# A group of products split in three, state-space chunks five tiles apart, and bias loads moved behind the last chunk's inputs

## The chip, the cores and the metric

The kernel runs on one core of a Trainium2 chip. The metric is the device time of one execution in microseconds. A core has five engines that run their own instruction streams and meet at semaphores: TensorE (PE, with its weight loads as PEld), VectorE (DVE), ScalarE (ACT), GpSimd (POOL), and SyncE (SP), which here only issues DMAs. ScalarE issues a few DMAs too.

## The reference, cut to what matters

Two transformer blocks over 256 tokens of 2048 channels, all in float32. The first block projects the normed input into queries, keys and values of a neighbourhood attention, a state-space input and memory queries; the three mixers' outputs are normed, joined and projected, and an MLP follows. The second block has four other mixers, its own out-projection and MLP.

```python
proj = h @ w_in                       # h = rmsnorm(x), 256 x 2048
q_na, k_na, v_na, u_ssm, q_mem = split(proj, [1024, 2048, 3072, 3584])
# neighbourhood attention: scores + bias table na_rpb, window 8 x 16 of a 64-wide grid
s = einsum('bqhd,bqkhd->bhqk', q_blk, k_g) * scale + rpb_flat[:, bidx]
# state space, 32 groups x 64 states, both directions: h_t = lam_bar * h_(t-1) + b_bar u_t
bu = einsum('bsgc,gpc->bsgp', u, b_bar)
_, h = associative_scan(combine, (a, bu), reverse=reverse)
y  = einsum('bsgp,gcp->bsgc', h, c).real
y  = gelu(y_f + y_b + d * u); y = y * sigmoid(y @ w_glu + b_glu)
# memory attention: q_mem against keys and values of 256 memory rows
x = x + rmsnorm(concat(norm(y_na), norm(y_ssm), norm(y_mem)) @ w_out)
x = x + rmsnorm(square(relu(rmsnorm(x) @ w_ff1)) @ w_ff2)
```

## The kernel before

Everything is one program with an order written out by hand for each engine. Weights stream through a ring of four 1 MB slots (`raw_weights`), loaded by SP in the order of `STREAM`. A product is done in one of two ways. **Unsplit** (`group`): float32 weights straight from the ring. **Split** (`group3`, `split_group`): ScalarE rounds a slot (`round_slot`, two halves, into `w_high`), VectorE takes the rest (`low`, two halves, into `w_low`), and PE does three products for each, high by high, low by high and high by low; x must be split too (`x_rounded` on ScalarE, `x_lower` on VectorE). `w_high` and `w_low` hold two slots each.

A group of 512 columns has 16 tiles of K, four to a slot. The first block's groups after the state-space input u come in this order, with the tiles counted through:

| tiles | group | form before |
|---|---|---|
| 0 to 15 | q0 | unsplit |
| 16 to 31 | k0 | unsplit |
| 32 to 47 | qm (memory queries) | unsplit |
| 48 to 63 | q1 | split |
| 64 to 79 | k1 | split |
| 80 to 111 | v0, v1 | split |

Between tiles PE calls `steps()`, which fits in the state space's work and the attention units. The state space runs in eight chunks i: `bu(i)` on PE after tile 2 + 6i; VectorE turns its result with sine and cosine tables, scans two parts of 512 (L2688), and turns back (h(i)); `ssm_y(i)` on PE; `yev(i)` on VectorE. bu(i) waits for yev(i-2), the scans for `decays(i)` on ScalarE, which waits for the scans of i-1; `tables(i)` on ScalarE waits for h(i-2) and for GpSimd's `turns`. y(i) stands after tiles 11, 17, ... 41, then 49 and 58. After y(7) come a gelu (VectorE, a tanh on ScalarE) and the gate's product.

`na_loads` on ScalarE issues 17 DMAs: a mask, and 16 pieces of the bias table of 128 KB each in rows of 64 floats, into `na_bias`, which lies over the residual. GpSimd then adds the mask to the eight heads' bias (L2080). VectorE first reads the result at attention unit 4, whose step is after tile 86.

ScalarE's order around these, before:

```python
angles(4); na_loads(); decays(2); tables(3)
...
tables(7); x_rounded(0); x_rounded(1); round_slot("q1", 0); decays(7)
act.wait_ge(pe_done, at("bu", CHUNKS - 1))
round_slot("q1", 1); x_rounded(2); x_rounded(3); evac("qm", qm)
```

The out-projections (`wout1`, `wout2`) begin with half slots (`left_half`), each over both token tiles, between which the last attention steps run; the first one waits, token tile by token tile, for the evacuation of the accumulators that it overwrites. After wout1 and ff2_1 the rows are copied out, squared and summed (`row_sums` on both engines), and PE turns them with a diagonal that ScalarE makes (L1451, PE's L832).

Of the kernel before, what the change touches and what calls it, by code (L numbers as in the profile page):

```python
# [7 lines left out]
P = 128  # L8
TT = S // P
# [14 lines left out]
CHUNKS = 8  # L24
HT = S // 2
# [30 lines left out]
STREAM += [(g, 4, False, 1) for g in ("q0", "k0", "qm")]  # L56
STREAM += [("q1", 4, True, 1), ("k1", 4, True, 1), ("glu", 1, False, 1), ("v0", 4, True, 1), ("v1", 4, True, 1), ("wout1", 16, True, 0), ("ff1_1", 64, True, 16), ("ff2_1", 64, True, 0)]
# [75 lines left out]
def program(nc, A, out, seen, book):  # L133
# [5 lines left out]
    with ctx:  # L139
# [48 lines left out]
        bbarE, cdE = tiles(place("x_behind", 22528, 2048), 0, 16, P), R(16640, 64, 32)  # L188
# [4 lines left out]
        angle = [tuple(tiles(scratch, 6144 + 1024 * b + 512 * i, 4, HT) for i in range(2)) for b in range(2)]  # L193
# [4 lines left out]
        na_mask = region[:, 1024:1536]  # L198
# [394 lines left out]
        PERIOD = 6  # L593
# [7 lines left out]
        def _(pe):  # L601
# [87 lines left out]
            def split_group(name, form="wide", between=None):  # L689

                acc_free(name)
                for j in range(KT // SK):
                    k = SPLIT_OF[SLOT0[name] + j]
                    state["n"] += 1
                    if name == "q1":
# [305 lines left out]
            def left_half(k, n, pos, first, free=None, order=(0, 1)):  # L1001
# [3 lines left out]
                for t in order:  # L1005
                    if free is not None:
                        pe.wait_ge(*free[t])
                    for c in range(2):
                        last = out_product(pos, t, c, wh[:, 512 * c:512 * c + 512], wl[:, 512 * c:512 * c + 512], first)
                last.then_inc(*((half_done, 1) if n == 0 else (split_used, 1)))  # L1010

# [32 lines left out]
            def wout1():  # L1044

                k, a0 = SPLIT0["wout1"], ACC0["wout1"]

                def scores_read():
                    pe.wait_ge(dve_done, at("scaled", U1 - 1))

                def last_value():
                    attend1(U1 + 2)

                def near_sums():
                    pe.wait_ge(act_done, at("out", U1 - 1))
# [8 lines left out]
                left_half(k, 0, 0, True, [(acc_freed, a0), (acc_freed, a0 - 1)], (1, 0))  # L1064
                attend1(U1 - 1)
                left_half(k, 1, 1, False)
                attend1(U1)
                left_half(k + 1, 0, 2, False)
                attend1(U1 + 1)
                left_half(k + 1, 1, 3, False)  # L1070
# [116 lines left out]
            for g in ("q0", "k0", "qm"):  # L1187
                group(g, xn, between=steps)
            for g in ("q1", "k1"):
                split_group(g, between=steps)  # L1190
# [157 lines left out]
            def wout2():  # L1348

                k = SPLIT0["wout2"]  # L1350

                def scores_read():
                    pe.wait_ge(dve_done, at("window", "sumread"))

                def nothing():
                    pass

                def forget_sums():
                    pe.wait_ge(act_done, at("out2", ND - 1))
# [6 lines left out]
                left_half(k, 0, 0, True, [(act_done, at("evac", "fva")), (act_done, at("evac", "fvb"))])  # L1366
                duo_step(TAIL0)
                pe.wait_ge(dve_done, at("scaled2", ND - 1))
                norm("window", xo, [gathered("window", 0, 4), gathered("window", 1, 8)], bank=4)
                left_half(k, 1, 1, False)  # L1370
# [24 lines left out]
        def _(act):  # L1395
# [57 lines left out]
            def row_sums(name, product):  # L1453

                row_copy(name, product, 0, 1, True)
                row_copy(name, product, 0, 3, True)
                row_root(name, 0)
                row_copy(name, product, 1, 1, True)
# [280 lines left out]
            acc_done("memv")  # L1739
            angles(0)  # L1740
# [35 lines left out]
            def na_loads():  # L1776

                act.wait_ge(dve_done, at("x", "out"))
                act.wait_ge(dve_done, at("cd_stepped"))
# [26 lines left out]
            na_loads()  # L1806
# [30 lines left out]
            evac("q1", q1[:, 4:8])  # L1837
# [264 lines left out]
        def _(dve):  # L2102
# [49 lines left out]
            def row_sums(name, product, after, eps=None):  # L2152

                row_copy(name, product, 0, 0, True)
                slot_half(after, 0, 0)
                row_copy(name, product, 0, 2, True)
                row_factor(name, 0, eps)
                row_copy(name, product, 1, 0, True)
                row_copy(name, product, 1, 2, True)
                row_factor(name, 1, eps)  # L2160

            def row_copies(name, product, after):

                row_copy(name, product, 0, 0, False)
                slot_half(after, 0, 0)
                row_copy(name, product, 0, 2, False)
                row_copy(name, product, 1, 0, False)
                row_copy(name, product, 1, 2, False)

# [487 lines left out]
            def x_lower(c):  # L2657

                dve.wait_ge(act_done, at("x", "high", c))
                dve.wait_ge(pe_done, at("slot", SLOT0["qm"] + c))  # L2660
# [40 lines left out]
            x_lower(2)  # L2701
            low("q1", 2)
            x_lower(3)
# [172 lines left out]
            for (g, j), (nxt, q) in zip(WOVEN_SLOTS, AHEAD):  # L2876
                ticks = TICKS[g, j]
                for slot, name, x in ((("sq", 1), "nq", nq), (("fk", 1), "fq", fq)):
                    if (g, j) == slot:
                        dve.wait_ge(act_done, at("evac", name))  # L2880
                        tt(x, x, by_keys(4), ALU.mult, name + "_scaled")
                for c, p in enumerate(ticks):
# [8 lines left out]
                    duo_normal(p)  # L2891
                    if p == FOX0:
# [120 lines left out]
```

## Time and profile before

| | |
|---|---|
| median of 3 runs | 2266.74 us (2266.41 to 2266.82) |
| the profiled execution's own time | 2266.6 us |
| its span | 2264.8 us |
| PE busy | 2238.2 us, 99% |
| VectorE, ScalarE busy | 1332.2 us (59%), 1040.4 us (46%) |
| GpSimd busy | 94.0 us (4%) |
| granted clock of PE | 1.00 of full speed in the whole span |
| 50 to 300 us: busy in each 50 us | PE 49.52, 50.00, 50.00, 50.00, 50.00; VectorE 45.03, 41.39, 41.63, 35.13, 26.43 |

A busy time is the union of an engine's instructions. Matmuls overlap, so the step from one to the next is the time that one costs, not its own duration. "[3.38 <-PE ps L914]" behind an instruction says that its engine was idle for 3.38 us before it and what ended the wait. "ACTq" and "SPq" are the queues' DMA issues.

### The profile page before, as it was taken

The page shows a single profiled execution, that of the slowest core. Times are in us where ns is not written, and L with a number is a line of the kernel's source. Part 1 is how long each engine was busy: PE and PEld are TensorE (multiplying, and loading weights), DVE is VectorE, ACT ScalarE, POOL GpSimd, SP SyncE. Part 2 cuts the span into 40 slices and gives each one's busy share as a digit, 9 for nine tenths or more (in the row PEclk, how much of TensorE's full clock was granted, in tenths as well). Part 3 has the DMA queues.
Part 4 walks back from the last instruction along what each step waited for, and adds up shares of the span by engine and source line. Part 5 has one row for each costly group of instructions (what it writes and reads, how often), then busy time and mean ns, then how long its engine had stood idle before and what let it go on. Part 6 is the DMA issues. An engine that isn't in the chain of part 4 may idle for free.

```text
span 2264.8 us, 32839 instructions
## 1 busy us (share of the span) xinstructions
PE 2238.2 (99%) x13276; PEld 1918.9 (85%) x13276; DVE 1332.2 (59%) x1548; ACT 1040.4 (46%) x1453; POOL 94.0 (4%) x66
## 2 busy tenths in 40 slices
PE   8999999999999999999999999999999999999998
PEld 7888988888888888888898988888888888888887
DVE  6878665764545545444486578847545455454445
ACT  6433564543434444444464466636434344444444
POOL 0552000000000000000000000000000000000000
PEclk9999999999999999999999999999999999999999
DMA  8364436566666555565544433355666665555553
GB/s 322 128 155 153 149 130 228 154 186 185 185 185 185 187 196 193 206 239 186 195 158 139 165 113 113 131 195 158 186 185 185 185 185 187 202 186 194 194 188 109
DMA packets 153513, 402.32 MB, mean 178 GB/s; under 512 B 15296, under 2 KB 30912, under 8 KB 133200
## 3 DMA queue, kind: packets, MB, share of 16 engines
q1 hardware_dynamic: 142112, 394.83, 53.0%
q10 hardware_dynamic: 11312, 6.22, 1.2%
q8 instruction: 65, 1.06, 0.2%
q14 instruction: 24, 0.20, 0.0%
HBM read 398.90 MB, written 2.13 MB: 177 GB/s over the span
## 4 chain that ended last, share of the span: by engine, by line
PE 93%; DVE 4%; ACT 2%; issue 1%; DMA 0%; SPq 0%; ACTq 0%; DVEq 0%
PE ps L757 21%; PE ps L758 11%; PE ps L795 10%; PE ps L797 10%; PE ps L796 10%; PE ps L620 5%; PE ps L628 3%; PE ps L629 3%; PE ps L630 3%; PE ps L997 2%; PE ps L999 2%; PE ps L998 2%; PE ps L642 1%; PE ps L644 1%; PE ps L643 1%
## 5 line engine op out<-in xcount | busy, mean ns | idle before, releaser
L2284 DVE TENSOR_TENSOR w_low<-raw_weights,w_high 128x1024 fp32r<-128x1024 f32 x659 | 776.4, 1218 | 782.5 <-ACT w_high L1487 778.3
L1487 ACT ACTIVATE w_high<-raw_weights 128x1024 fp32r<-128x1024 f32 (+1 forms) x634 | 634.7, 1049 | 817.0 <-PE ps L797 398.5
L757 PE MATMUL ps<-x_split,w_high 128*128 128x512 f32 x2048 | 725.3, 399 | 1.7 <-DVE x_split L2272 1.7
L758 PE MATMUL ps<-x_split,w_low 128*128 128x256 f32 x2048 | 575.2, 281 | 0.0
L757 PEld LDWEIGHTS ps<-x_split,w_high 128*128 128x128 f32 x2048 | 384.8, 188 | 98.4 <-issue 3.0
L795 PE MATMUL ps<-w_high,x_split 128*128 128x512 f32 x1024 | 398.4, 389 | 0.0
L797 PE MATMUL ps<-w_high,x_split 128*128 128x512 f32 x1024 | 398.4, 389 | 0.0
L796 PE MATMUL ps<-w_low,x_split 128*128 128x512 f32 x1024 | 398.4, 389 | 0.0
L758 PEld LDWEIGHTS ps<-x_split,w_low 128*128 128x128 f32 x2048 | 386.9, 189 | 0.0
L797 PEld LDWEIGHTS ps<-w_high,x_split 128*128 128x128 f32 x1024 | 192.3, 188 | 40.2
L796 PEld LDWEIGHTS ps<-w_low,x_split 128*128 128x128 f32 x1024 | 192.3, 188 | 39.7
L795 PEld LDWEIGHTS ps<-w_high,x_split 128*128 128x128 f32 x1024 | 192.3, 188 | 39.7
L629 PE MATMUL ps<-x_split,w_high 128*128 128x256 f32 x544 | 153.8, 283 | 0.0
L628 PE MATMUL ps<-x_split,w_high 128*128 128x256 f32 x416 | 121.4, 292 | 0.8 <-DVE x_split L2272 0.4
L630 PE MATMUL ps<-x_split,w_low 128*128 128x256 f32 x416 | 117.5, 283 | 0.0
L620 PE MATMUL ps<-x_over_high,raw_weights 128*128 128x256 f32 x512 | 115.0, 382 | 0.0
L620 PEld LDWEIGHTS ps<-x_over_high,raw_weights 128*128 128x128 f32 x512 | 95.9, 190 | 14.6 <-issue 1.2
L629 PEld LDWEIGHTS ps<-x_split,w_high 128*128 128x128 f32 x544 | 104.2, 192 | 0.2
L997 PE MATMUL ps<-w_high,x_split 128*128 128x512 f32 x256 | 101.4, 396 | 2.8 <-ACT region L1926 1.6
L999 PE MATMUL ps<-w_high,x_split 128*128 128x512 f32 x256 | 99.7, 390 | 0.0
L998 PE MATMUL ps<-w_low,x_split 128*128 128x512 f32 x256 | 99.7, 389 | 0.0
L1523 ACT ACTIVATE region<-ps 128x1024 f32 (+1 forms) x32 | 32.9, 1027 | 116.1 <-PE ps L758 116.1
(298 smaller groups left out, 2321.5 us busy)
## 6 DMA issues: line engine op xcount, KB each, us to landing
raw_weights<-in_w_ff SPq DMA_DIRECT2D x128, 1024.0 KB, 5.6
raw_weights<-in_w_up SPq DMA_DIRECT2D x64, 1024.0 KB, 5.7
raw_weights<-in_w_down SPq DMA_DIRECT2D x64, 1024.0 KB, 4.8
raw_weights<-in_w_in SPq DMA_DIRECT2D x62, 1024.0 KB, 5.4
raw_weights<-in_w_out SPq DMA_DIRECT2D x32, 1024.0 KB, 4.8
raw_weights<-in_w_mem_kv SPq DMA_DIRECT2D x7, 1024.0 KB, 14.6
residual<-in_xT SPq DMA_DIRECT2D x2, 2048.0 KB, 14.4
region<-t_table ACTq DMA_DIRECT2D x1, 3072.0 KB, 16.6
```

The costliest lines, as they stand in the source:

```text
L620: last = nc.tensor.matmul(acc[:, c], w[:, P * c:P * c + P], x, start=(kt == 0 and c % 2 == 0), stop=(kt == kts - 1), skip_group_check=True)
L628: nc.tensor.matmul(o, h, xh_, start=(first and c % 2 == 0), stop=False, skip_group_check=True)
L629: nc.tensor.matmul(o, h, xl_, start=False, stop=False, skip_group_check=True)
L630: last = nc.tensor.matmul(o, wl[:, P * c:P * c + P], xh_, start=False, stop=done, skip_group_check=True)
L757: nc.tensor.matmul(o, wh[:, q, w], xs[:, kt], start=(kt == 0), stop=False, skip_group_check=True)
L758: last = nc.tensor.matmul(o[:, 0:S], wl[:, q, w], xh[:, kt], start=False, stop=(kt == KT - 1), skip_group_check=True)
L795: nc.tensor.matmul(o, h, wh[:, r], start=(first and j == 0), stop=False, skip_group_check=True)
L796: nc.tensor.matmul(o, h, wl[:, r], start=False, stop=False, skip_group_check=True)
L797: last = nc.tensor.matmul(o, l, wh[:, r], start=False, stop=True, skip_group_check=True)
L997: nc.tensor.matmul(o, h, wh, start=first, stop=False, skip_group_check=True)
L1487: nc.scalar.activation(split_slot(wh_t, k)[:, r], ring_slot(n)[:, r], ACT.Copy).then_inc(rounded, 1)
L2284: V.tensor_tensor(split_slot(wl_t, k)[:, r], ring_slot(n)[:, r], split_slot(wh_t, k)[:, r].bitcast(f32), ALU.subtract).then_inc(split_read ...
```

## The change

The memory queries' group (qm) becomes a split group. Its x is therefore split earlier, in place over xn as k0's slots are used up, and high x goes where `bbarE` was; `bbarE` and the angles move into the residual's place. With that, `na_loads` can only run when the last `bu` is done. The chunks' steps are listed anew: bu after 2, 7, 12, 17, 22, 27, 37, 47, y after 10, 15, 20, 25, 31, 42, 53, 62. Three more edits stand further on: both out-projections begin with `first_rows`, which does two half slots for one token tile and only then asks for the second accumulator; the half slot that VectorE lowers amid the row copies moves behind them, and ScalarE copies one more row piece ahead of the first root; the scaling of nq and fq moves behind a tick's normalising.

```diff
-STREAM += [(g, 4, False, 1) for g in ("q0", "k0", "qm")]
-STREAM += [("q1", 4, True, 1), ("k1", 4, True, 1), ...
+STREAM += [(g, 4, False, 1) for g in ("q0", "k0")]
+STREAM += [("qm", 4, True, 1), ("q1", 4, True, 1), ("k1", 4, True, 1), ...
...
-        bbarE, cdE = tiles(place("x_behind", 22528, 2048), 0, 16, P), R(16640, 64, 32)
+        bbarE, cdE = tiles(xres_t, 0, 16, P), R(16640, 64, 32)
-        angle = [tuple(tiles(scratch, 6144 + 1024 * b + 512 * i, 4, HT) ...
+        angle = [tuple(tiles(xres_t, 2048 + 1024 * b + 512 * i, 4, HT) ...
-        na_mask = region[:, 1024:1536]
+        na_mask = mix_t[:, 1024:1536]
...
-        BU_AFTER = {2 + PERIOD * i: i for i in range(CHUNKS)}
-        Y_AFTER = {**{11 + PERIOD * i: i for i in range(CHUNKS - 2)}, 49: CHUNKS - 2, 58: CHUNKS - 1}
+        BU_AFTER = dict(zip((2, 7, 12, 17, 22, 27, 37, 47), range(CHUNKS)))
+        Y_AFTER = dict(zip((10, 15, 20, 25, 31, 42, 53, 62), range(CHUNKS)))
...
+            def first_rows(k, order, free, between):
+                for i, t in enumerate(order):
+                    pe.wait_ge(*free[t])
+                    for n in range(2):
+                        if i == 0:
+                            pe.wait_ge(split_ready, 2 * k + n + 1)
+                        wh, wl = (split_slot(x, k)[:, HALF * n:HALF * n + HALF] for x in (wh_t, wl_t))
+                        for c in range(2):
+                            last = out_product(n, t, c, ..., n == 0)
+                    if i == 0:
+                        last.then_inc(half_done, 1)
+                        between()
+                last.then_inc(split_used, 1)
...
             # ScalarE
             acc_done("memv")
+            act.wait_ge(dve_done, at("x", "out"))
...
             angles(4)
-            na_loads()
             decays(2)
...
             angles(6)
+            for c in range(4):
+                x_rounded(c)
             decays(4)
             tables(5)
             angles(7)
+            round_slot("qm", 0)
             decays(5)
+            round_slot("qm", 1)
             tables(6)
             evac("k0", k1[:, 0:4])
+            round_slot("qm", 2)
             decays(6)
+            round_slot("qm", 3)
             tables(7)
-            x_rounded(0)
-            x_rounded(1)
             round_slot("q1", 0)
+            act.wait_ge(pe_done, at("bu", CHUNKS - 1))
+            na_loads()
+            evac("qm", qm)
+            round_slot("q1", 1)
             decays(7)
-            act.wait_ge(pe_done, at("bu", CHUNKS - 1))
-            round_slot("q1", 1)
-            x_rounded(2)
-            x_rounded(3)
-            evac("qm", qm)
             round_slot("q1", 2)
             round_slot("q1", 3)
             round_slot("k1", 0)
+            evac("q1", q1[:, 4:8])
             act.wait_ge(dve_done, at("gelu_in"))
             ... Tanh ...
-            act.wait_ge(pool_done, at("na_masked"))
-            evac("q1", q1[:, 4:8])
...
             # VectorE, chunk loop
+                if i == CHUNKS - 3:
+                    x_lower(0)
+                    low("qm", 0)
+                if i == CHUNKS - 2:
+                    x_lower(1)
+                    low("qm", 1)
+                    x_lower(2)
+                    low("qm", 2)
                 if i == CHUNKS - 1:
-                    x_lower(0)
                     low("q1", 0)
...
                     (scans of chunk i)
+                if i == CHUNKS - 2:
+                    x_lower(3)
+                    low("qm", 3)
                 if i == CHUNKS - 1:
-                    x_lower(1)
                     low("q1", 1)
                 if i:
                     yev(i - 1)
```

## Rows read from the trace of the kernel before

**Rows 1.** The page, busy times; and a group's total and mean ns of one.

```profile
PE 2238.2 (99%) x13276; PEld 1918.9 (85%) x13276; DVE 1332.2 (59%) x1548; ACT 1040.4 (46%) x1453; POOL 94.0 (4%) x66
...
L1487 ACT ACTIVATE w_high<-raw_weights 128x1024 fp32r<-128x1024 f32 (+1 forms) x634 | 634.7, 1049 | 817.0 <-PE ps L797 398.5
```

**Rows 2.** PE's waits, whole span: us in total, times, longest.

```profile
PE ps L628 <- DVE mem_low L2514: 7.6, 1, 7.6
PE ps L832 <- ACT rinv L1451: 3.7, 4, 1.3
...
PE ps L997 <- ACT region L1926: 1.6, 1, 1.6
PE ps L1110 <- DVE region L2445: 1.1, 1, 1.1
PE ps L997 <- ACT region L1513: 0.8, 1, 0.8
```

**Rows 3.** Chain that ended last, 150 to 250 us: start, us, what.

```profile
176.24 5.38 PE ps L620 x24
181.61 1.14 PE ps L914 x32
...
188.13 0.36 PE ps L928 x8
188.50 1.88 PE ps L934 x64
...
204.41 0.12 PE ps L628
...
204.65 0.12 PE ps L630
```

**Rows 4.** Timeline of VectorE, 60 to 175 us: start, us, what.

```profile
117.02 2.63 DVE L2688 TENSOR_TENSOR_SCAN mixed<-mixed 128x512 f32<-128x512 f32 x2
...
154.56 1.29 DVE L2107 TENSOR_TENSOR region<-ps,region 128x512 f32<-128x512 f32 x2 [3.21 <-PE ps L914]
...
159.06 2.34 DVE L2688 TENSOR_TENSOR_SCAN region<-mixed,region 128x512 f32<-128x512 f32 x2
...
164.02 1.29 DVE L2107 TENSOR_TENSOR region<-region 128x512 f32<-128x512 f32 x2
168.69 1.29 DVE L2107 TENSOR_TENSOR region<-ps,region 128x512 f32<-128x512 f32 x2 [3.38 <-PE ps L914]
```

**Rows 5.** Timeline of ScalarE and its queue, 60 to 260 us.

```profile
111.69 0.33 ACTq L1780 DMA_DIRECT2D region<-in_na_mask  x1
...
114.84 13.30 ACTq L1786 DMA_DIRECT2D residual<-in_na_rpb  x12
128.19 0.63 ACT L1768 ACTIVATE mixed<-rinv 128x508 f32<-128x508 f32 x1 [13.44 <-DVE region L2107]
```

**Rows 6.** The line of the bias loads: ns min/median/max.

```profile
L1786 ACTq DMA_DIRECT2D residual<-in_na_rpb x16: 642/672/3517, 112.1 to 127.5; - x16
```

**Rows 7.** Timelines of GpSimd and VectorE, 166 to 290 us.

```profile
171.37 13.95 POOL L2080 TENSOR_TENSOR residual<-residual,region 128x512 f32<-128x512 f32 x8
...
173.22 4.33 DVE L2688 TENSOR_TENSOR_SCAN mixed<-mixed 128x512 f32<-128x512 f32 x2
...
180.86 3.31 DVE L2107 TENSOR_TENSOR mixed<-region,mixed 128x512 f32<-128x512 f32 x2
```

**Rows 8.** Timelines of VectorE and ScalarE, 222 to 233 us.

```profile
222.82 0.42 DVE L2107 TENSOR_TENSOR mixed<-ps,mixed 128x256 f32<-128x256 f32 x1 [3.07 <-PE ps L934]
225.57 2.36 DVE L2284 TENSOR_TENSOR w_low<-raw_weights,w_high 128x1024 fp32r<-128x1024 f32 x2 [2.32 <-ACT w_high L1487]
...
229.83 1.23 DVE L2107 TENSOR_TENSOR region<-region,mixed 128x1024 f32<-128x1024 f32 x1
...
231.09 1.06 ACT L1835 ACTIVATE region<-region 128x1024 f32<-128x1024 f32 x1 [3.31 <-DVE region L2107]
232.05 1.01 ACT L1513 ACTIVATE region<-ps 128x1024 f32<-128x1024 f32 x1
```

More of the change, by code:

```diff
@@ L55 @@
 STREAM = [("memk", 4, True, 1), ("memv", 4, True, 1), ("u", 4, False, 1)]
-STREAM += [(g, 4, False, 1) for g in ("q0", "k0", "qm")]
-STREAM += [("q1", 4, True, 1), ("k1", 4, True, 1), ("glu", 1, False, 1), ("v0", 4, True, 1), ("v1", 4, True, 1), ("wout1", 16, True, 0), ("ff1_1", 64, True, 16), ("ff2_1", 64, True, 0)]
+STREAM += [(g, 4, False, 1) for g in ("q0", "k0")]
+STREAM += [("qm", 4, True, 1), ("q1", 4, True, 1), ("k1", 4, True, 1), ("glu", 1, False, 1), ("v0", 4, True, 1), ("v1", 4, True, 1), ("wout1", 16, True, 0), ("ff1_1", 64, True, 16), ("ff2_1", 64, True, 0)]
 STREAM += [("mla_c", 4, True, 0), ("small", 2, True, 0), ("nk", 4, True, 0), ("uqa", 1, False, 0), ("uqb", 1, False, 0),
@@ L192, in program @@
         decay_f = mix_t[:, 0:4 * HT]
-        angle = [tuple(tiles(scratch, 6144 + 1024 * b + 512 * i, 4, HT) for i in range(2)) for b in range(2)]
+        angle = [tuple(tiles(xres_t, 2048 + 1024 * b + 512 * i, 4, HT) for i in range(2)) for b in range(2)]
         same_step = mix_t[:, 2048 - 256:2048].rearrange("p (i c) -> p i c", c=32)
@@ L592, in program @@
         GAINS_OF = {"mlp": "mlp_pre"}
-        PERIOD = 6
         TURN_AFTER = 0
-        BU_AFTER = {2 + PERIOD * i: i for i in range(CHUNKS)}
-        Y_AFTER = {**{11 + PERIOD * i: i for i in range(CHUNKS - 2)}, 49: CHUNKS - 2, 58: CHUNKS - 1}
+        BU_AFTER = dict(zip((2, 7, 12, 17, 22, 27, 37, 47), range(CHUNKS)))
+        Y_AFTER = dict(zip((10, 15, 20, 25, 31, 42, 53, 62), range(CHUNKS)))
         UNITS_AFTER = {70 + 4 * i: i for i in range(11)}
@@ L694, in split_group @@
                     state["n"] += 1
-                    if name == "q1":
+                    if name == "qm":
                         pe.wait_ge(dve_done, at("x", "low", j))
@@ L999, in out_product, with left_half @@
                 return nc.tensor.matmul(o, l, wh, start=False, stop=True, skip_group_check=True)
-            def left_half(k, n, pos, first, free=None, order=(0, 1)):
+            def left_half(k, n, pos, first):
                 pe.wait_ge(split_ready, 2 * k + n + 1)
                 wh, wl = (split_slot(x, k)[:, HALF * n:HALF * n + HALF] for x in (wh_t, wl_t))
-                for t in order:
-                    if free is not None:
-                        pe.wait_ge(*free[t])
+                for t in range(TT):
                     for c in range(2):
@@ L1010, in left_half @@
                 last.then_inc(*((half_done, 1) if n == 0 else (split_used, 1)))
+            def first_rows(k, order, free, between):
[6 more added lines that the diff above has]
+                        for c in range(2):
+                            last = out_product(n, t, c, wh[:, 512 * c:512 * c + 512], wl[:, 512 * c:512 * c + 512], n == 0)
+                    if i == 0:
+                        last.then_inc(half_done, 1)
+                        between()
+                last.then_inc(split_used, 1)
             def right_halves(k, pos, first, before=()):
@@ L1063, in wout1 @@
                 pe.wait_ge(dve_done, at("memn", "sumread"))
-                left_half(k, 0, 0, True, [(acc_freed, a0), (acc_freed, a0 - 1)], (1, 0))
+                first_rows(k, (1, 0), [(acc_freed, a0), (acc_freed, a0 - 1)], lambda: None)
                 attend1(U1 - 1)
-                left_half(k, 1, 1, False)
+                left_half(k + 1, 0, 2, False)
                 attend1(U1)
-                left_half(k + 1, 0, 2, False)
+                left_half(k + 1, 1, 3, False)
                 attend1(U1 + 1)
-                left_half(k + 1, 1, 3, False)
                 right_halves(k + 2, 0, True, [scores_read, last_value, near_sums, near_read])
@@ L1185, in steps @@
                     norm("memn", early_sq, [gathered("memn", 0, 4)], bank=3)
-            for g in ("q0", "k0", "qm"):
+            for g in ("q0", "k0"):
                 group(g, xn, between=steps)
-            for g in ("q1", "k1"):
+            for g in ("qm", "q1", "k1"):
                 split_group(g, between=steps)
@@ L1365, in wout2, with step_and_sums @@
                 pe.wait_ge(dve_done, at("group", "out", 0))
[L1366 to L1370, printed above, removed]
+                def step_and_sums():
+                    duo_step(TAIL0)
+                    pe.wait_ge(dve_done, at("scaled2", ND - 1))
+                    norm("window", xo, [gathered("window", 0, 4), gathered("window", 1, 8)], bank=4)
+                first_rows(k, (0, 1), [(act_done, at("evac", "fva")), (act_done, at("evac", "fvb"))], step_and_sums)
                 duo_step(TAIL0 + 1)
@@ L1456, in row_sums @@
                 row_copy(name, product, 0, 3, True)
+                row_copy(name, product, 1, 1, True)
                 row_root(name, 0)
-                row_copy(name, product, 1, 1, True)
                 row_copy(name, product, 1, 3, True)
@@ L1776, in na_loads @@
             def na_loads():
-                act.wait_ge(dve_done, at("x", "out"))
-                act.wait_ge(dve_done, at("cd_stepped"))
                 act.dma_start(na_mask, A["na_mask"]).then_inc(na_loaded, 16)
@@ L2154, in row_sums @@
                 row_copy(name, product, 0, 0, True)
-                slot_half(after, 0, 0)
                 row_copy(name, product, 0, 2, True)
+                row_copy(name, product, 1, 0, True)
                 row_factor(name, 0, eps)
-                row_copy(name, product, 1, 0, True)
                 row_copy(name, product, 1, 2, True)
                 row_factor(name, 1, eps)
+                slot_half(after, 0, 0)
             def row_copies(name, product, after):
                 row_copy(name, product, 0, 0, False)
-                slot_half(after, 0, 0)
                 row_copy(name, product, 0, 2, False)
@@ L2168, in row_copies @@
                 row_copy(name, product, 1, 2, False)
+                slot_half(after, 0, 0)
             def rows(name, product, scale=None):
@@ L2659, in x_lower @@
                 dve.wait_ge(act_done, at("x", "high", c))
-                dve.wait_ge(pe_done, at("slot", SLOT0["qm"] + c))
+                dve.wait_ge(pe_done, at("slot", SLOT0["k0"] + c))
                 tt(x_low[:, 4 * c:4 * c + 4], xn[:, 4 * c:4 * c + 4], x_high[:, 4 * c:4 * c + 4].bitcast(f32), ALU.subtract, "x", "low", c)
@@ L2700, in _ @@
                 tt(gi, cs, gi, ALU.mult, "h", i)
-            x_lower(2)
             low("q1", 2)
-            x_lower(3)
             low("q1", 3)
@@ L2877, in _ @@
                 ticks = TICKS[g, j]
[L2878 to L2881, printed above, removed]
                 for c, p in enumerate(ticks):
@@ L2891, in _ @@
                     duo_normal(p)
+                    for slot, name, x in ((("sq", 1), "nq", nq), (("fk", 1), "fq", fq)):
+                        if (g, j) == slot and c == 0:
+                            dve.wait_ge(act_done, at("evac", name))
+                            tt(x, x, by_keys(4), ALU.mult, name + "_scaled")
                     if p == FOX0:
```

## The prediction, written before the kernel ran

> **What bounds the kernel now.** I read the busy times first: TensorE (PE) is busy for 99% of the span [rows 1], so a microsecond counts only where PE loses or gains it. Next, who waited for whom on PE [rows 2]: some 20 us in all, of which 7.6 us is at the very start, which the change leaves alone, and nothing between 100 and 300 us, the stretch of the projections with the state-space chunks. There the chain that ended last runs through PE matmul by matmul [rows 3]. So the change can gain by giving PE less to do, or by removing one of the small waits of rows 2; it can lose by making PE wait where it doesn't now. I therefore follow the other engines through that stretch [rows 4 to 8].
>
> **The memory queries' group, split.** An unsplit tile of K (8 recorded matmuls, L620) takes PE 5.38 / 3 = 1.79 us; a split tile has 12 matmuls, one each 0.12 us, 1.44 us [rows 3]. Sixteen tiles: 16 x (1.79 - 1.44) = **5.6 us less**. Its roundings on ScalarE (two halves of 1.05 us for each of 4 slots [rows 1]) and the low halves on VectorE (2.36 us a slot [rows 8]) are new work beside PE.
>
> **The chunks five tiles apart.** One period was six tiles, one bu and one y: 10.76 + 1.14 + 2.24 = 14.1 us; the same sum with five tiles is 12.3 us. VectorE's chain of a chunk runs from 154.56 to 165.3 and then waits 3.38 us for the next bu [rows 4]: 10.8 us, so 1.5 us of cover is left. yev(i-1), for which bu(i+1) waits, comes 8.2 us after bu(i) (three tiles, y, and the sum itself) and is wanted two tiles behind that y, at 11.2 us. I cost this at nothing. If one chunk ran as long as the 15.5 us of the one beside GpSimd's mask adds (168.69 to 184.2 [rows 4, 7]), it would cost 3.2 us once; but those adds stand elsewhere now.
> VectorE now lowers x and qm's slot 0 (1.2 + 2.4 us) before chunk 5, slots 1 and 2 before chunk 6. Counted from tile 27's end: chunk 5 starts at 3.3, waits for y(4) (after tile 31) till 10.5, ends at 13.8; x's part and the first low half are done at 16.2. PE, with y(4) behind it at 10.5, comes to tile 36 four split tiles later, at 16.3. So 0 to 1 us; I take 0.3.
> ScalarE's new wait for x ahead of angles(0) costs nothing: the angles already stand behind sines whose inputs VectorE makes after x.
>
> **The bias loads behind the last inputs.** This decides. bbarE and the angles now lie where the bias goes, so the loads must wait for the last bu. Before, `na_loads` stood at 111.7 us, where nobody was in a hurry. Its 17 issues kept ScalarE from starting anything: decays(2) had its input at 119.65 (the scans' end [rows 4]), but began at 128.19, right after the last issue, 13.44 us idle [rows 5]. One bias issue takes 0.67 us, some up to 3.5 us when transfers pile up [rows 6]. All 17 took from 111.69 to 128.14: 16.45 us; at the undisturbed rate they'd take 0.33 + 16 x 0.68 = 11.2 us.
> Now they wait for bu(7), which PE does after tile 47, and queued behind them on ScalarE are evac("qm"), round_slot("q1", 1) and decays(7); behind decays(7) are VectorE's last scans, and behind these its low("q1", 1). PE wants that slot at tile 52, four split tiles or 5.8 us after bu(7). Counted from bu(7)'s end: issues to 11.3; evacuation and its marker 1.2 [rows 8], to 12.5; rounding two halves, to 14.5; decay 0.6 [rows 5], to 15.1; scans 2.34 [rows 4], to 17.5; the first low half 1.2, to 18.7. PE stalls for 18.7 - 5.8 = **12.9 us** at least; with 16.45 us of issues, 18.2 us. The weight loads beside it are fewer than before (one slot, the rest wait for low halves), so I take 12.5 us of issues: 14.2 us. Then GpSimd's eight mask adds (13.95 us [rows 7]) start as the loads land, some 4 us after the last issue, so about when the scans run. Beside them before, two scans took 4.33 us in place of 2.34, and the two last products of h 3.31 in place of 1.29 [rows 4, 7]. Bounds 0 to 2.7 us; as these adds nearly coincide, 2.6. **First stall 16.8 us** (12.9 to 20.9).
> Had the issues cost nothing, VectorE's own path (four reads and two sums 4.4, scans 2.3, low half 1.2, with gaps 8.2 us) would still leave 2.4 us, since bu(7) is now only four tiles ahead of the slot.
> The Trainium skill speaks against this count: "DMA: Bandwidth & Descriptors", section "Issuing engines are not separate DMA queues", calls the time of starting a DMA on its sequencer usually small beside the DMA. By that rule the first stall would be the 2.4 us above and the whole 2262.6 us (rival 2); by the row's 13.44 us of a stopped engine it is what I forecast, and I go by the row.
>
> **y(6) and y(7) four tiles later.** VectorE waits for y(6) (yev), then finishes h(7), then lowers q1's slot 2: 0.5 + 2.7 + 1.2 = 4.4 us after y(6) [rows 4, 8]. PE has two tiles (2.9 us) until tile 56, before it had six. **Second stall 1.6 us**, up to 5.6 us if all of h falls beside GpSimd's adds; I take 2.7, since they end about then.
> y(7) now stands after tile 62. VectorE: yev 0.42, low("k1", 0) 2.36, three gelu operations 3.2 (227.9 to 231.06), tanh 1.06 on ScalarE, then round_slot("k1", 1) 1.05 and the low half 1.2 [rows 1, 8]: about 9.5 us after y(7). PE wants that half at tile 68, five tiles or 7.2 us later (nine before, 13 us); k1's first half is itself 0.3 us late. **Third stall 2.2 us** (1.5 to 3).
> Moving the wait for the masked bias out of evac("q1")'s way gains nothing; ScalarE didn't wait there. Its place is VectorE's scale1(4), at tile 86, over 30 us after the adds.
>
> **The edits further on.** `first_rows` does both slot halves of one token tile before it asks for the other accumulator. At wout2 this puts six products of 512 columns (estimate 1.4 us: as many columns as a split tile's twelve of 256), a duo step and the sums ahead of the wait for fvb's evacuation: the 1.6 us [rows 2] goes, less 0.1 for the slot's second half, which is ready just then: 1.5. At wout1 the 0.8 us goes. attend1(11) comes some 2.7 us later and its value is wanted as before; I estimate no new wait, 0.5 us at worst. `row_sums` without the low half in its midst: the 3.7 us in four waits for the diagonals [rows 2]: the low half's 1.2 us leaves VectorE's chain, but a row copy enters ahead of the first factor on both engines. I estimate the first diagonal 0.4 us later, which PE's turning of that half passes on, and the second, which PE waited for up to 1.3 us, 0.7 us earlier net, twice: 1.4 (bounds -1, if only the delay counts, and 3.7, the row). In `row_copies` PE didn't wait; the low half at the end meets a 1.1 us gap: 0.1 lost. The query scaling behind the tick takes 1.2 us out of the way of a duo scale: 1.1 us [rows 2]. Sum **4.7 us less** (2 to 7).
>
> **Sum.** -5.6 + 0.3 + 16.8 + 2.7 + 2.2 - 4.7 = +11.7 us. On the profiled execution's 2266.6 us (span 2264.8 and 1.8 around it; the median is 2266.74) this gives 2278.3 us, **2278.4** against the median, 0.5% more.
>
> **Rivals.**
> (1) *Issues blocked, as forecast*, with its ends: lows -5.6 + 12.9 + 1.6 + 1.5 - 7 = +3.4, highs -5.6 + 3.2 + 1 + 20.9 + 5.6 + 3 - 2 = +26.1; with the ends not all together 2271 to 2287. Chance 0.83.
> (2) *Issues hidden* (the other side): ScalarE gets through the 17 issues in under some 3 us and the path is VectorE's. For it: the mask's issue takes only 0.33 us [rows 5]. Against it: sixteen of 0.67 us or more [rows 6], and the idle engine. -5.6 + 2.4 + 1.6 + 2.2 - 4.7 = -4.1: 2262.6. The sign turns where the first stall is 5.5 us (5.6 + 4.7 - 4.8), that is with about 4 us of issues. Chance 0.07.
> (3) *The tail edits gain nothing* and the issues take their full 16.45 us, with GpSimd in every step: 2266.7 - 5.6 + 1 + 20.9 + 5.6 + 3 = 2291.6. Against it: each wait of rows 2 has its cause in what is moved. Chance 0.04.
> (4) *The stall is made up*: PE runs into the memory and gate parts with all slots ready and the small waits behind vanish. There are none between 100 and 300 us to vanish, so it could only be that all of rows 2's waits behind 300 us go (3.7 + 1.6 + 1.1 + 0.8 = 7.2 us) and the issues take 11.2 us without GpSimd's part: -5.6 + 12.9 + 1.6 + 2.2 - 7.2 = +3.9: 2270.6. Chance 0.06.
>
> Slower by over 0.2% (4.5 us, about what a measurement of this kernel can tell from no change) has (1) nearly whole (0.81), (3) and half of (4): 0.88. Within 0.2% the rest of (1) and (4) and a third of (2), whose -4.1 lies near the bound: 0.07. Faster, the rest of (2): 0.05. The range that leaves out 2 in 10 goes from 2269 to 2287; it leaves out (2), (3) and edges of (1).
>
> **What the profile after would show.** ScalarE's queue issuing 17 transfers right behind the last bu, with 11 to 16 us of idle time ahead of the next activation; one PE wait of 13 to 21 us for w_low (or w_high) at a split group's line, near 205 us; two waits of 1 to 5 us there, the last just before tanh's successor slot; L620's 128 matmuls fewer and 192 split ones more; the waits for L1926 and L1513 gone. Wrong would make it: a second ScalarE path that lets roundings pass the issues, or low("q1", 1) taken ahead of the scans.

## The result and the profile after

The changed kernel takes **2279.15 us** in the median of six runs (2276.52 to 2283.99), the kernel before 2266.48 us in six beside it (2266.36 to 2266.82): ratio 1.0065, interval 1.0052 to 1.0078. Slower by 0.65%; forecast were 2278.4 us and slower. The profiled execution took 2283.37 us, with a span of 2281.6 us, 16.8 us over that of before.

The medians must be read with care: both kernels have two times some 6 us apart, since the second block's first MLP product, which the change doesn't touch, runs that much shorter in some executions (its high products, L756, take 356.6 us between 1500 and 1900 us in the traces of runs 3 and 7, and 362.4 in that of run 6), three of the six of after (2276.5 to 2277.1) and none of the six of before. Like against like the change costs about 16.6 us (run 8, below).

PE's waits over the whole span (us in total, times, longest):

```profile
PE ps L627 <- DVE w_low L2296: 20.9, 6, 16.7
PE ps L627 <- DVE mem_low L2526: 8.1, 1, 8.1
...
PE ps L831 <- ACT rinv L1463: 1.7, 2, 0.9
PE ps L1094 <- DVE region L2119: 1.0, 1, 1.0
PE ps L996 <- DVE w_low L2296: 1.0, 1, 1.0
PE ps L927 <- DVE region L2119: 0.9, 1, 0.9
...
PE ps L1121 <- DVE region L2457: 0.4, 1, 0.4
```

The first line is new, and it is the change: 20.9 us of waits for low halves in the projections, 16.7 of them in one wait. Against [rows 2], the diagonals' wait (L831) has gone from 3.7 us in four to 1.7 in two, L1121's from 1.1 to 0.4, and both waits of the out-projections for evacuated accumulators are gone, but L996 now waits 1.0 us for a low half, and y(4) (L927) 0.9 us.

ScalarE and its queue behind the last bu, 195 to 230 us (start, us, what; in brackets the engine's idle time before it):

```profile
199.16 0.34 ACTq L1791 DMA_DIRECT2D mixed<-in_na_mask  x1
199.53 11.95 ACTq L1797 DMA_DIRECT2D residual<-in_na_rpb  x16
211.52 1.02 ACT L1525 ACTIVATE region<-ps 128x1024 f32<-128x1024 f32 x1 [17.22 <-issue]
...
212.68 1.99 ACT L1499 ACTIVATE w_high<-raw_weights 128x1024 fp32r<-128x1024 f32 x2
214.58 0.61 ACT L1781 ACTIVATE mixed<-rinv 128x508 f32<-128x508 f32 x1
```

The chain of the first stall stands here as forecast: 17 issues in 12.3 us, then evacuation, rounding, decay. Of the 17.22 us in which ScalarE was idle, 4.9 us went by before the first issue, in the wait for bu(7) (its last rounding had ended at 194.30 us); the rest is issuing. VectorE goes on from there, with GpSimd's adds beside it (first fence VectorE, second GpSimd, third PE):

```profile
215.28 4.22 DVE L2707 TENSOR_TENSOR_SCAN mixed<-mixed 128x512 f32<-128x512 f32 x2 [12.06 <-ACT mixed L1781]
219.43 4.43 DVE L2296 TENSOR_TENSOR w_low<-raw_weights,w_high 128x1024 fp32r<-128x1024 f32 x2
```

```profile
215.02 13.68 POOL L2092 TENSOR_TENSOR residual<-residual,mixed 128x512 f32<-128x512 f32 x8 [47.86 <-DMA residual<-in_na_rpb]
```

```profile
204.75 0.28 PE L629 MATMUL ps<-x_high,w_low 128*128 128x256 f32 x1
...
221.69 0.58 PE L627 MATMUL ps<-x_high,w_high 128*128 128x256 f32 x1 [16.66 <-DVE w_low L2296]
222.07 0.42 PE L628 MATMUL ps<-x_split,w_high 128*128 128x256 f32 x1
222.29 0.42 PE L629 MATMUL ps<-x_high,w_low 128*128 128x256 f32 x1
```

The two scans took 4.22 us and the low halves 4.43, where pairs without GpSimd beside them took 2.34 [rows 4] and 2.36 [rows 8]. PE, stopped for 16.66 us, starts again with steps of 0.21 us from matmul to matmul, where [rows 3] had 0.12. The reason is in the granted clock of the same stretch (window, its length, PE busy with the count, granted clock, DMA share, GB/s):

```profile
208.00:209.00 1.00, 0.00 (x0) 1.00 1.15 179
209.00:210.00 1.00, 0.00 (x0) 0.77 1.19 194
210.00:211.00 1.00, 0.00 (x0) 0.50 1.19 161
...
225.00:226.00 1.00, 1.00 (x7) 0.50 0.78 145
226.00:227.00 1.00, 1.00 (x10) 0.70 0.91 334
227.00:228.00 1.00, 1.00 (x36) 1.00 1.04 406
```

PE's last matmul ends near 205.0. The clock falls to 0.50 of full speed (1.2 of 2.4 GHz) between 209 and 210, while PE stands still, and comes back between 226 and 227, after it has worked again since 221.69. That made some 22 matmuls 0.09 us slower each: 2.1 us on top of the stall.

**Where the 16.8 us went**, by the starts of the same step in both traces: tile 48's second matmul starts at 199.24 instead of 202.22 us, with the same work done before it in both lists (bu up to 7, y up to 5), so PE is 3.0 us ahead there. The first attention unit starts at 259.79 instead of 240.05: 19.7 us behind, so 22.7 us were lost in between (waits of 16.7, 1.3 and 1.5 us, the clock's 2.1, and 1.2 that are left over, for restarts and tiles). From there to the end 2.9 us came back. -3.0 + 22.7 - 2.9 = +16.8.

### The profile page after: what moved, and what is told of

Its sections match the earlier page's. It is cut to its first block, busy times and chain, and to the rows that moved or that the text cites. A ratio compares the mean times of both kernels' runs of the same rounds, so it can differ in the third digit from the quotient of the medians.

```text
span 2281.6 us, 32986 instructions
## 1 busy us (share of the span) xinstructions
PE 2237.2 (98%) x13340; PEld 1921.1 (84%) x13340; DVE 1344.2 (59%) x1556; ACT 1048.0 (46%) x1461; POOL 97.1 (4%) x66
## 4 chain that ended last, share of the span: by engine, by line
PE 87%; DVE 4%; ACT 1%; issue 1%; ACTq 1%; DVEq 0%
PE ps L756 21%; PE ps L757 11%; PE ps L795 10%; PE ps L796 10%; PE ps L794 10%; PE ps L627 3%; PE ps L628 3%; PE ps L629 3%; PE ps L996 2%; PE ps L997 2%; PE ps L998 2%; PE ps L641 1%; PE ps L643 1%; PE ps L642 1%; DVE w_low L2296 1%; PE ps L1094 1%
## 5 line engine op out<-in xcount | busy, mean ns | idle before, releaser
L2296 DVE TENSOR_TENSOR w_low<-raw_weights,w_high 128x1024 fp32r<-128x1024 f32 (+1 forms) x667 | 788.5, 1222 | 773.6 <-ACT w_high L1499 769.6
L1499 ACT ACTIVATE w_high<-raw_weights 128x1024 fp32r<-128x1024 f32 x642 | 642.6, 1049 | 831.8 <-PE ps L796 398.5
L756 PE MATMUL ps<-x_split,w_high 128*128 128x512 f32 x2048 | 725.3, 399 | 1.7 <-DVE x_split L2284 1.7
L756 PEld LDWEIGHTS ps<-x_split,w_high 128*128 128x128 f32 x2048 | 384.8, 188 | 98.3 <-issue 3.0
L628 PE MATMUL ps<-x_split,w_high 128*128 128x256 f32 x608 | 172.8, 284 | 0.0
L627 PE MATMUL ps<-x_split,w_high 128*128 128x256 f32 x416 | 121.4, 292 | 0.8 <-DVE x_split L2284 0.4
L628 PEld LDWEIGHTS ps<-x_split,w_high 128*128 128x128 f32 x608 | 117.5, 193 | 0.2
L996 PE MATMUL ps<-w_high,x_split 128*128 128x512 f32 x256 | 101.2, 395 | 1.2 <-DVE w_low L2296 1.0
L619 PE MATMUL ps<-x_over_high,raw_weights 128*128 128x256 f32 x384 | 86.3, 382 | 0.0
L627 PEld LDWEIGHTS ps<-x_split,w_high 128*128 128x128 f32 x416 | 79.5, 191 | 5.7 <-issue 4.4
```

The costliest lines, as they stand in the source:

```text
L627: nc.tensor.matmul(o, h, xh_, start=(first and c % 2 == 0), stop=False, skip_group_check=True)
L628: nc.tensor.matmul(o, h, xl_, start=False, stop=False, skip_group_check=True)
L756: nc.tensor.matmul(o, wh[:, q, w], xs[:, kt], start=(kt == 0), stop=False, skip_group_check=True)
L996: nc.tensor.matmul(o, h, wh, start=first, stop=False, skip_group_check=True)
L1499: nc.scalar.activation(split_slot(wh_t, k)[:, r], ring_slot(n)[:, r], ACT.Copy).then_inc(rounded, 1)
L2296: V.tensor_tensor(split_slot(wl_t, k)[:, r], ring_slot(n)[:, r], split_slot(wh_t, k)[:, r].bitcast(f32), ALU.subtract).then_inc(split_read ...
```

## The experiments

Each is the changed kernel with one edit, where nothing else is said. "Before" in a comparison is the kernel before on the same chip.

**1. GpSimd issues the loads.** The stall's cause should be ScalarE's issuing, not the loads' late place.

```diff
 # ScalarE
-            act.wait_ge(pe_done, at("bu", CHUNKS - 1))
-            na_loads()
 # GpSimd, ahead of its mask adds
+            pool.wait_ge(pe_done, at("bu", CHUNKS - 1))
+            na_loads()   # the same 17, on pool.dma_start
```

> The changed kernel, but GpSimd issues the 17 loads behind bu(7) in place of ScalarE. Theory (ScalarE's queue blocked by the issues for 12.3 us makes the first stall): the first PE wait falls from 16.7 us to about 2.4 us, PE keeps its full clock there, the waits of 1 to 2 us behind y(6) and y(7) stay: 2279.2 - 14.3 - 2.1 = 2263 us. Rival (GpSimd's mask adds or the transfers themselves hold VectorE up, whoever issues): the stall stays over 10 us, 2275 us or more.

Measured: 2265.6 us (2259.79 to 2267.32, ten runs), before 2266.04; ratio 0.9992 (0.9981 to 1.0003). GpSimd's timeline:

```profile
199.56 0.78 POOL L2079 DMA_DIRECT2D mixed<-in_na_mask  x1 [32.29 <-PE ps L913]
200.34 10.92 POOL L2085 DMA_DIRECT2D residual<-in_na_rpb  x16
219.15 10.70 POOL L2088 TENSOR_TENSOR residual<-residual,mixed 128x512 f32<-128x512 f32 x8 [7.89 <-DMA residual<-in_na_rpb]
```

The same loads at the same time, issued nearly as slowly (11.7 us), on an engine for which nobody waits: the 16.66 us wait shrinks to 1.73 us, and the clock stays at 1.00 there. So it was ScalarE's being blocked, and not the transfers. (GpSimd's adds no longer meet the two scans either, which are back at 2.34 us: they start at 219.15, when VectorE is past them.) The loss of the whole change is gone, but it gains nothing yet, 2.6 us short of the 2263 expected: PE still waits 1.73 + 1.28 + 0.29 + 1.49 us between 205 and 240 us.

**2. Half the pieces.** Eight of the sixteen bias pieces are loaded; the rest of the bias isn't there.

```diff
-                for r in range(S // GRID_W):
+                for r in range(2):
...
-            pool.wait_ge(na_loaded, 16 * 17)
+            pool.wait_ge(na_loaded, 16 * 9)
```

> The changed kernel with 8 of the 16 bias pieces loaded (the rest of the bias table stays unset, so half of the attention's bias is not the reference's). Theory: ScalarE is blocked for 0.34 + 8 x 0.67 = 5.7 us in place of 12.3, so the first stall is 6 to 7 us shorter, near 10 us; with the clock lost as now 2272.5 us, without that loss 2270.4. Rival (the issues are hidden, the stall is VectorE's or the transfers'): within 1 us of the changed kernel.

Measured: 2276.9 us (2270.22 to 2277.4, seven runs), ratio 1.0051 (1.0035 to 1.0066), with the stall and the clock of its trace (ScalarE's queue; PE; windows of PE):

```profile
199.38 6.45 ACTq L1797 DMA_DIRECT2D residual<-in_na_rpb  x8
205.87 1.02 ACT L1525 ACTIVATE region<-ps 128x1024 f32<-128x1024 f32 x1 [11.71 <-PE ps L629]
```

```profile
215.53 0.58 PE L627 MATMUL ps<-x_high,w_high 128*128 128x256 f32 x1 [10.65 <-DVE w_low L2296]
```

```profile
208.00:209.00 1.00, 0.00 (x0) 1.00 0.00 0
209.00:210.00 1.00, 0.00 (x0) 0.60 0.03 8
```

Eight issues fewer end 5.65 us sooner, and the stall is 6.0 us shorter: the stall follows the issues nearly one for one. Like against like (most runs near 2277 against run 8's 2282.8) the time is 5.9 us less. The 2272.5 expected was worked out from the median of both kinds, 2279.15, and so came out too low. The clock fell at the same moment and cost a little less, some 1.6 us: 17 matmuls at the slow step, until 219.5 us.

**3. The same 17 issues on ScalarE, later in its list.** What is queued behind them is changed, not their number.

```diff
+            decays(7)
+            evac("qm", qm)
+            round_slot("q1", 1)
             act.wait_ge(pe_done, at("bu", CHUNKS - 1))
             na_loads()
-            evac("qm", qm)
-            round_slot("q1", 1)
-            decays(7)
```

> The changed kernel with ScalarE's order decays(7), evac(qm), round_slot(q1, 1), wait for bu(7), na_loads in place of the loads ahead of the three. Theory: the same 12 us of issues, but nothing that PE needs soon stands behind them; q1's slot 2 would be ready some 15.4 us after bu(7) and is wanted at 16. First stall 2.4 us, second 1.3 to 2.5: 2263 to 2265 us. Rival (the length of the issues or the transfers beside the products counts, not the order): 2275 us or more.

Measured: 2265.5 us (2258.82 to 2267.49, ten runs), ratio 0.9995 (0.9982 to 1.0008). ScalarE:

```profile
198.42 1.04 ACT L1499 ACTIVATE w_high<-raw_weights 128x1024 fp32r<-128x1024 f32 x1
198.43 0.34 ACTq L1791 DMA_DIRECT2D mixed<-in_na_mask  x1
...
199.54 15.15 ACTq L1797 DMA_DIRECT2D residual<-in_na_rpb  x15
214.79 3.90 ACT L1499 ACTIVATE w_high<-raw_weights 128x1024 fp32r<-128x1024 f32 x4 [14.38 <-PE ps L629]
```

ScalarE is blocked for as long as before and longer (15.15 us for 15 issues), but the one stall of 16.66 us has become 1.73 us, and the one at q1's slot 2 is 2.69 us now. The price of an issue is what stands queued behind it.

**4. The later edits alone**: the kernel before, with `first_rows`, the row copies and the query scaling of the change.

> The kernel before with only the edits behind the first block's projections (first_rows at both out-projections, the row copies' order, the scaling behind the tick). By the prediction 4.7 us less: 2261.8 us. By the trace after (0.8 + 1.6 + 2.0 + 0.7 of waits gone, a new 1.0 at w_low and 0.3 at the first fox tick): 2.9 to 3.8 less, 2263 us. Rival (they gain nothing): 2266.5.

Measured: 2262.25 us (2257.39 to 2263.53, ten runs), ratio 0.9988 (0.9977 to 0.9999): 3.8 us less than before, where the prediction had 4.7. PE's waits there:

```profile
PE ps L832 <- ACT rinv L1464: 1.7, 2, 0.9
...
PE ps L997 <- DVE w_low L2297: 1.0, 1, 1.0
```

The wait for the evacuation at wout1 turned into one for the slot's low half.

**5. One mask add instead of eight** (seven heads stay without their mask), for GpSimd's part in the stall.

```diff
-            for h in range(NA_HEADS):
+            for h in range(1):
```

> The changed kernel, with GpSimd adding the mask to one head's bias instead of eight (seven heads of the near attention stay without their mask). If GpSimd's adds lengthened VectorE's scans and low half beside them (4.22 and 4.43 us for pairs that took 2.34 and 2.36 elsewhere), the first wait for a low half falls from 16.7 us to about 14.5 (two scans and one low half, -1.9 and -1.1, if the one add stands beside none of them) and the whole by 2.5 to 3 us. The rival: they are long for another reason (the transfers, code), and the wait stays at 16.7. TensorE's clock falls all the same, since its idle stretch stays over 10 us.

Measured: 2281.01 us (2278.68 to 2282.53, five runs), 1.8 us under the unaltered kernel in the same batch (2282.8). VectorE and PE:

```profile
214.68 3.35 DVE L2707 TENSOR_TENSOR_SCAN mixed<-mixed 128x512 f32<-128x512 f32 x2 [12.07 <-ACT mixed L1781]
217.95 2.33 DVE L2296 TENSOR_TENSOR w_low<-raw_weights,w_high 128x1024 fp32r<-128x1024 f32 x2
```

```profile
219.20 0.58 PE L627 MATMUL ps<-x_high,w_high 128*128 128x256 f32 x1 [14.79 <-DVE w_low L2296]
```

The one add, at 214.56 to 215.83 us, met the scans, and they are still 1.0 us longer than the 2.34 of [rows 4]; the low halves are back at 2.33. The stall is 1.9 us shorter and the time 1.8, of 2.5 to 3 expected, so the adds do lengthen VectorE's work, by not far from what the prediction put in (2.6, with all eight). In the trace after, the two scans and the first low half are 1.9 + 1.0 us longer than alone. The Trainium skill ("SBUF — State Buffer", section "SBUF: two separate sides") says that a VectorE operation with two SBUF inputs and a GpSimd operation that reads SBUF exclude each other on a shared pair of ports. Pairs of scans and of low halves of nearly double length beside the adds (4.22 and 4.43 us against 2.34 and 2.36) agree with it.

**6 and 7. The places.** With GpSimd issuing, bu(7), y(6) and y(7) get back the distances that they had before; the second kernel also makes the last decay first and moves y(4) one tile.

```diff
-        BU_AFTER = dict(zip((2, 7, 12, 17, 22, 27, 37, 47), range(CHUNKS)))
-        Y_AFTER = dict(zip((10, 15, 20, 25, 31, 42, 53, 62), range(CHUNKS)))
+        BU_AFTER = dict(zip((2, 7, 12, 17, 22, 27, 37, 45), range(CHUNKS)))
+        Y_AFTER = dict(zip((10, 15, 20, 25, 31, 42, 49, 58), range(CHUNKS)))
 # the second kernel: y(4) after 32, and on ScalarE
+            decays(7)
             evac("qm", qm)
             round_slot("q1", 1)
-            decays(7)
```

> GpSimd issues the loads, and the last state and the last two outputs of the state-space chunks stand where the kernel before had them in distance: bu(7) behind tile 45 instead of 47, y(6) behind 49 instead of 53, y(7) behind 58 instead of 62. With GpSimd issuing and the places as changed TensorE waited 1.73 + 1.28 + 0.29 + 1.49 us in this stretch. If these waits come from the distances of the places, all four go, in the profile and in the time: about 2260.5 to 2261.5 against 2265.6. The rival: ScalarE's order behind bu(7) (an evacuation and a rounding ahead of the decay) keeps the first wait at some 1 us, and the other restarts cost as much: 2263 to 2265.

> As the one before, and ScalarE makes the last chunk's decay ahead of qm's evacuation and q1's second rounding, and y(4) stands behind tile 32 instead of 31. If a wait was left of the first, it goes now, and so does the 0.95 us wait for y(4) at 168 us: 2259.5 to 2261, the fastest of all, some 5.5 us below the kernel before. The rival: y(4)'s wait only moves to qm's next slot, and the time is that of the run before.

Measured: 2262.41 us (2262.14 to 2264.16, eleven runs; ratio 0.9984, 0.9975 to 0.9993) and 2262.47 us (2256.7 to 2264.11, eleven runs; 0.9985, 0.9976 to 0.9994). Against run 1's median 3.2 us came (some 4 against its six longer runs, 2265.24 to 2267.32), of four to five expected, and the second kernel's edits, expected to bring 2259.5 to 2261, added nothing. The second kernel's waits in this stretch:

```profile
176.41 0.36 PE L627 MATMUL ps<-x_high,w_high 128*128 128x256 f32 x1 [1.35 <-DVE w_low L2292]
234.76 0.39 PE L627 MATMUL ps<-x_high,w_high 128*128 128x256 f32 x1 [2.14 <-DVE w_low L2292]
```

The waits at q1 are gone. y(4)'s 0.94 us only moved on to qm's slot 1 (0.31 us before, 1.35 now), which was the rival. And k1's slot 1, behind tanh, is late by 2.14 us for another reason than y(7)'s place: VectorE waits 2.32 us for k1's rounded slot 0 ahead of the gelu.

**8. The changed kernel again.**

> The changed kernel, unaltered, to see how its times spread: its six had 2276.5 to 2277.1 three times and 2281.2 to 2284.0 three times, the kernel before 2266.4 to 2266.8 in its six, but some 2260 in six of 28 later ones. If both kernels have two times some 6 us apart with like shares, ten runs have both here, the lower near 2276.7 and the upper near 2282.5, and like against like the change costs about 16 to 17 us. If the upper values were a chance of that chip, all are near 2277 and it costs 10.5 to 11.

Measured: 2282.8 us (2282.22 to 2283.22, five runs) against 2266.22 (2265.74 to 2266.8, 21 runs); ratio 1.0072 (1.0058 to 1.0086), a difference of 16.6 us. All runs of both are near the longer of the two times here, so this is the comparison of like with like, and it agrees with the 16.8 us between the two traces. Why a program has two times, with other shares in other batches, stays open.

**9 and 10. Two places in VectorE's list**, both on top of run 7's kernel. The gelu goes ahead of k1's first low half; then qm's slot 1 behind chunk 5's scans.

```diff
             yev(CHUNKS - 1)
-            low("k1", 0)
             ... gelu_in ...
+            low("k1", 0)
             low("k1", 1)
 # the second kernel, chunk loop
                 if i == CHUNKS - 2:
-                    x_lower(1)
-                    low("qm", 1)
...
                     (scans of chunk i)
+                if i == CHUNKS - 3:
+                    x_lower(1)
+                    low("qm", 1)
```

> The fastest kernel so far (GpSimd issues, places as far apart as before, the last decay first), with VectorE making gelu's input right behind y(7) and k1's slot 0 after it. In its profile a wait of 2.14 us was left at 234.8 us, for k1's slot 1, whose rounding stands behind tanh; gelu's input stood behind k1's first low half, which waits for a split buffer. If that order makes the wait, it goes: about 2 us less, 2260.3 against 2262.5. The rival: the rounding waits for its split buffer or k1's slot 0 comes late in exchange, and 0 to 1 us is gained.

> As the one before, and qm's slot 1 is lowered behind chunk 5's scans instead of ahead of chunk 6. The 1.35 us wait for it at 176.4 us goes if the place in VectorE's list makes it: 2259 against 2260.3. The rival: its rounding on ScalarE comes no earlier, or y(5) and bu(6) are late in exchange: no gain over the run before.

Measured: 2260.41 us (2253.85 to 2261.55, nine runs; ratio 0.9968, 0.9958 to 0.9978) and **2258.86 us** (2258.36 to 2260.41, six runs; 0.9967, 0.9955 to 0.9979), before 2266.16. Both came out as expected, 2.1 and 1.5 us less. The last kernel has one wait left between 97 and 240 us:

```profile
226.69 0.36 PE L627 MATMUL ps<-x_high,w_high 128*128 128x256 f32 x1 [1.12 <-ACT region L1525]
```

It is the fastest, 7.3 us below the kernel before, and 3.4 us below the later edits alone: that is what splitting qm gives with this one wait left. In its trace PE starts y(6) at 200.49 instead of 205.06 us, 4.6 us ahead.

## Why the prediction was right

The number was right to 0.75 us, and so was the mechanism of the main term, but part of the closeness is luck: like against like the change costs 16.6 us, not 11.7, and the terms were off in both directions. One by one:

| term | predicted | measured |
|---|---|---|
| qm split and chunks, up to tile 48 | -5.3 | -3.0 |
| first stall | 16.8 | 16.7 |
| second and third stall | 2.7 + 2.2 | 1.3 + 1.5 |
| clock after the stall | not there | 2.1 |
| restarts, tiles (what is left over) | not there | 1.2 |
| later edits | -4.7 | -2.9 (alone, run 4: -3.8) |

- **qm split.** Off by 2.3 us. I forecast 0.3 us of delay; there were a 0.93 us wait for y(4) and 0.31 us at qm's slot 1. y(4) now asks for h(4) behind VectorE's work of chunk 4, which I costed at nothing because I checked only the chunk's 10.8 us against its period of 12.3 (measured 12.39), and not its end against y's place. Another 0.8 us is in the tile, 1.49 us in the mean of the sixteen (y(4) at 168.15 to bu(7) at 197.88, less the wait, two y and one bu) instead of 1.44; the rest, 0.6 us, I didn't follow. Run 10, without those waits, was 4.6 us ahead at y(6), of the 5.6.
- **First stall.** 17 issues took 12.3 us, forecast 12.5; the steps behind them came in the order and at the lengths written down; GpSimd's part was put at 2.6 us; the longer scans and low half of the trace after make 2.9, and run 5 measured 1.9 for seven of eight adds. Runs 1 to 3 separate the cause: without ScalarE's issuing 1.73 us is left (forecast: 2.4), with half of it 10.65, and with other work queued behind it 1.73. ScalarE's idle time was 17.22 us instead of 11 to 16, because I had left its wait for bu(7) out of it.
- **Rival (2), issues hidden**, is refuted by the 12.3 us of issuing in which ScalarE started nothing else, and by run 1. The Trainium skill ("DMA: Bandwidth & Descriptors", section "Issuing engines are not separate DMA queues") says that the time to start a DMA on the sequencer is usually small beside the DMA. Load by load the trace after agrees: 0.66 us for an issue against 4.0 us from issue to landing, both in the median. But that the issues are therefore hidden doesn't follow from it: seventeen in a row are 12.3 us for whatever is queued behind them. The rival's 2262.6 us would have needed what runs 1 and 3 did; these ended at 2265.6, as the split's gain was smaller than its term.
- **Second and third stall** were forecast too large by 1.4 and 0.7 us. GpSimd's adds ran until 228.7 us, and y(6)'s first read by VectorE came at 229.29, so that the adds met none of the work behind it, for which I had put in 1.1 us.
- **The later edits.** The diagonals gave 2.0 us of their 3.7 in the waits and 2.4 us in the time (442.51 to 1165.79 us in the trace after is 723.3 us, the same stretch before, 422.46 to 1148.20, 725.7), above the 1.4 forecast. wout1's 0.8 us was given back by a new 1.0 us wait for the low half: I had checked the slot's second half at wout2, where it was ready, and not at wout1. Run 4 measured all of them together at 3.8 us; why only 2.9 us shows in the trace after stays open.
- **The clock** is the step that was missing. The granted clock of the trace of before reads 1.00 in the whole span, and I didn't ask what a long stop does to it. But PE's steps there show what a restart costs. Behind its first wait, of 7.61 us, they are 0.21 us, as at the low clock behind the stall, and 0.12 us only from 13.27 us on:

```profile
7.61 0.55 PE L628 MATMUL ps<-mem_high,w_high 128*128 128x256 f32 x1 [7.61 <-DVE mem_low L2514]
...
8.39 0.41 PE L628 MATMUL ps<-mem_high,w_high 128*128 128x256 f32 x1
8.61 0.41 PE L629 MATMUL ps<-mem_low,w_high 128*128 128x256 f32 x1
8.82 0.41 PE L630 MATMUL ps<-mem_high,w_low 128*128 128x256 f32 x1
...
13.27 0.28 PE L630 MATMUL ps<-mem_high,w_low 128*128 128x256 f32 x1
13.39 0.28 PE L628 MATMUL ps<-mem_high,w_high 128*128 128x256 f32 x1
```

  Those are 24 slow steps, 2.2 us at 0.09 us each, and that could have gone into the sum beside a forecast stall of 16.8 us. The lengths of the steps say more here than the clock's rows, which read 1.00 even in these first microseconds; that the clock was low there is inferred from the steps.

Rival (3) fell with the later edits' gain, rival (4) with the size of the loss.

## What to carry to other kernels

A DMA issue costs its engine the time of the issue, and everything behind it in that engine's list: before moving issues to a place where the data's deadline allows it, ask what is queued behind them and when PE wants it; if the answer is "soon", give them to an engine with nothing to do, or put them behind the urgent work. When an edit leaves fewer tiles between a producer and its consumer, check the producer's end against the new place, for each one, not only its work against its period. A change that moves several places can hold a gain under its loss: here the waits of the trace, removed one by one, led from 16.6 us slower to 7.3 us faster.

## What the runs showed of the hardware that I hadn't expected

- The granted clock of TensorE fell to 0.50 (1.2 of 2.4 GHz) in the middle of a wait: between 209 and 210 us in the trace after and in runs 2 and 5, near 210 in run 8, with PE's last matmul ended near 205.0. In the trace after it was still 0.50 at 225 to 226 us, though PE had worked again since 221.69. Matmul steps were 0.21 us in place of 0.12. After the waits of 1.7 us in runs 1 and 3 the steps were 0.12 us from the second matmul on.
- GpSimd needed 0.68 us for each bias load that it issued (10.92 / 16), ScalarE 0.75 (11.95 / 16, with a median of 0.66 and one of 1.60). So moving such loads to GpSimd doesn't make them cheap. What an issue costs differs by load on SP and ScalarE: 0.37 us for a weight load of 1 MB, 0.34 for the mask, 0.66 for a bias piece of 128 KB. On GpSimd the mask took 0.78 us, as long as a bias piece.
- An issue on ScalarE can take much longer than its median: 15.15 us for 15 of them in run 3, with the longest at 2.86 us, against 11.95 for 16 in the trace after. In run 3 the long ones (1.30 to 2.86 us, from 208.96 on) came behind a weight load that SP issued at 207.14; in the trace of before, those of 1.97 and 3.52 us (at 120.18 and 122.19) behind one issued at 117.54. That the weight load makes them long is likely, but no run varies it. GpSimd's issues in run 1 stayed at 0.76 us or less behind one issued at 208.00.
